# Scaling the delta rule's values on GpSimd instead of VectorE in a two-block fp32 transformer kernel

## The reference, cut to what matters

```python
qkv = jax.nn.silu(causal_short_conv(g_qkv, conv_w))
gq, gk, gv = jnp.split(qkv, [GDN_QK_DIM, 2 * GDN_QK_DIM], axis=-1)
gq = l2_normalize(gq.reshape(B, S, GDN_HEADS, GDN_HEAD_K)) * (GDN_HEAD_K ** -0.5)
gk = l2_normalize(gk.reshape(B, S, GDN_HEADS, GDN_HEAD_K))
beta = jax.nn.sigmoid(g_b.astype(jnp.float32))
...
k_beta = k * beta[..., None]
a_mat = jnp.where(strict, jnp.einsum('bhnid,bhnjd->bhnij', k_beta, k) * decay, 0.0)
lhs = a_mat + jnp.eye(C, dtype=f32)
rhs = jnp.concatenate([v * beta[..., None], k_beta * jnp.exp(g_cum)[..., None]], axis=-1)
sol = lax.linalg.triangular_solve(lhs, rhs, left_side=True, lower=True, unit_diagonal=True)
```

## Time and profile before

| | |
|---|---|
| time, median of 3 runs | 929.16 us (928.70 to 929.86) |
| profiled execution, its own time | 928.95 us |
| its span, first to last instruction | 927.0 us |
| PE busy | 896.3 us (97%) |
| DVE busy | 574.6 us (62%) |
| ACT busy | 511.9 us (55%) |
| POOL busy | 90.7 us (10%) |
| mean granted TensorE clock | 1.000 |

### The profile page before, as it was taken

One profiled execution on the slowest core, in us unless ns is written; L12 is line 12 of the kernel. 1 busy time (PEld: TensorE's weight loads), 2 busy tenths in 40 slices (PEclk: granted clock), 3 DMA queues, 4 the chain that ended last, 5 costly groups with the idle time before them and its releaser, 6 DMA issues. The chain is left out here.

```text
span 927.0 us, 14627 instructions
## 1 busy us (share of the span) xinstructions
PE 896.3 (97%) x5672; PEld 795.1 (86%) x5672; DVE 574.6 (62%) x903; ACT 511.9 (55%) x934; POOL 90.7 (10%) x113
## 2 busy tenths in 40 slices
PE   5999999999999999998999999998999999999998
PEld 5998977888899998887878889977899789998886
DVE  5446556664676664446657988889655676665333
ACT  4465666664665544336468668796255465554331
POOL 1010000000000000001000512240152101000000
PEclk9999999999999999999999999999999999999999
DMA  9756333464455565655454644353340365655552
GB/s 340 250 182 228 95 134 101 148 228 92 147 173 184 183 203 198 203 188 182 136 183 151 196 143 145 104 173 121 88 168 1 110 206 172 184 189 185 182 185 87
DMA packets 110379, 152.22 MB, mean 164 GB/s; under 512 B 6736, under 2 KB 68328, under 8 KB 109928
## 3 DMA queue, kind: packets, MB, share of 16 engines
q1 hardware_dynamic: 110312, 151.31, 50.5%
HBM read 147.99 MB, written 3.30 MB: 163 GB/s over the span
## 5 line engine op out<-in xcount | busy, mean ns | idle before, releaser
L400 DVE TENSOR_TENSOR s_w_lo<-s_w_raw,s_w_hi 128x2048 fp32r<-128x2048 f32 (+1 forms) x198 | 312.4, 1595 | 174.9 <-ACT s_w_hi L394 174.6
L394 ACT ACTIVATE s_w_hi<-s_w_raw 128x2048 fp32r<-128x2048 f32 (+1 forms) x198 | 262.8, 1346 | 152.7 <-PE acc L452 101.9
L462 PE MATMUL acc<-s_h_hi,s_w_hi 128*128 128x256 f32 x800 | 228.0, 285 | 1.9 <-DVE s_h_lo L686 1.9
L464 PE MATMUL acc<-s_h_hi,s_w_lo 128*128 128x256 f32 x800 | 226.3, 283 | 0.0
L463 PE MATMUL acc<-s_h_lo,s_w_hi 128*128 128x256 f32 x800 | 226.3, 283 | 0.0
L462 PEld LDWEIGHTS acc<-s_h_hi,s_w_hi 128*128 128x128 f32 x800 | 153.3, 192 | 2.7 <-DVE s_w_lo L400 1.2
L463 PEld LDWEIGHTS acc<-s_h_lo,s_w_hi 128*128 128x128 f32 x800 | 153.4, 192 | 0.3
L464 PEld LDWEIGHTS acc<-s_h_hi,s_w_lo 128*128 128x128 f32 x800 | 153.3, 192 | 0.0
L452 PE MATMUL acc<-s_w_hi,s_hid_lo 128*128 128x512 f32 x224 | 88.3, 394 | 0.0
L451 PE MATMUL acc<-s_w_lo,s_hid_hi 128*128 128x512 f32 x224 | 87.8, 392 | 0.0
L450 PE MATMUL acc<-s_w_hi,s_hid_hi 128*128 128x512 f32 x224 | 86.9, 388 | 0.0
(11 more groups left out here) (319 smaller groups left out, 1431.0 us busy)
## 6 DMA issues: line engine op xcount, KB each, us to landing
s_w_raw<-in_w_in SPq DMA_DIRECT2D x44, 1024.0 KB, 5.2
s_w_raw<-in_w_ff SPq DMA_DIRECT2D x32, 1024.0 KB, 5.1
s_w_raw<-in_w_mlp_up SPq DMA_DIRECT2D x16, 1024.0 KB, 5.5
s_w_raw<-in_w_mlp_down SPq DMA_DIRECT2D x16, 1024.0 KB, 5.0
s_w_raw<-in_w_out SPq DMA_DIRECT2D x8, 1024.0 KB, 5.3
s_w_raw<-in_w_mk SPq DMA_DIRECT2D x4, 1024.0 KB, 5.1
s_w_raw<-in_w_mv SPq DMA_DIRECT2D x4, 1024.0 KB, 5.0
s_w_raw<-in_w_mq SPq DMA_DIRECT2D x4, 1024.0 KB, 5.0
```

Source lines behind the costliest of these rows:

```text
L394: act.activation(w_hi[u % SPLIT_SLOTS][:, cs], w_raw[u % RAW_SLOTS][:, cs], ACT.Copy).then_inc(w_hi_done, 4 if q is None else 1)
L400: dve.tensor_tensor(w_lo[u % RAW_SLOTS][:, cs], w_raw[u % RAW_SLOTS][:, cs], w_hi[u % SPLIT_SLOTS][:, cs].bitcast(F32), ALU.subtract).then ...
L462: pe.matmul(o, wh[:, cs], hi[:, k, :], start=k == 0, stop=False)
L464: i = pe.matmul(o, wl[:, cs], hi[:, k, :], start=False, stop=k == KC - 1)
```

## The change

The two multiplications of `vb` by beta leave VectorE's stream. GpSimd does them, as the same two 128 x 1024 operations, after `tok_rms_pool(1)` and before `inv_pool`. They report on a semaphore of their own, `vb_done`, and TensorE waits for it before the first matmuls that read `vb`.

```diff
-            else:
-                dve.wait_ge(tok_copied, 12)
-                dve.tensor_tensor(vb[:, n], vb[:, n], per_head(BETA[:, n, :]), ALU.mult).then_inc(tok_done, 1)
+
+        def vb_pool(pool, n):
+            pool.wait_ge(tok_copied, 12)
+            pool.tensor_tensor(vb[:, n], vb[:, n], per_head(BETA[:, n, :]), ALU.mult).then_inc(vb_done, 1)
...
                 if k == 0:
+                    pe.wait_ge(vb_done, NT)
                     pe.wait_ge(u_copied, u_event(0, LEVELS, g))
...
             tok_rms_pool(pool, 1)
+            pool.wait_ge(g2_eg, 2)
+            for n in range(NT):
+                vb_pool(pool, n)
             for n in range(NT):
                 inv_pool(pool, n)
...
             gate_tick(6)
-            for k in range(4, 8):
+            for k in range(4, 6):
                 tok_scale_dve(dve, k)
             kdec_dve(dve)
```

More of the change, by code:

```diff
@@ L365, in build_program @@
         conv_done, conv2_done, tanh_done, qkv_done = [sem(n) for n in ("conv_done", "conv2_done", "tanh_done", "qkv_done")]
-        gate_tanh, tok_mm, tok_copied, tok_sq, tok_ss, tok_rms, tok_done = [sem(n) for n in (
-            "gate_tanh", "tok_mm", "tok_copied", "tok_sq", "tok_ss", "tok_rms", "tok_done")]
+        gate_tanh, tok_mm, tok_copied, tok_sq, tok_ss, tok_rms, tok_done, vb_done = [sem(n) for n in (
+            "gate_tanh", "tok_mm", "tok_copied", "tok_sq", "tok_ss", "tok_rms", "tok_done", "vb_done")]
         back_mm, back_copied, dt_add, dt_done, kdec_done, ap_mm, ap_done = [sem(n) for n in (
```

## The result

The changed kernel takes 931.35 us (median of 19 runs, 930.26 to 933.15) where before takes 929.47 us (19 runs, 927.96 to 931.22): ratio 1.0022, 95% interval 1.0015 to 1.0028, so slower by 0.22%; the two medians differ by 1.88 us. The profiled execution took 931.26 us, its span is 929.4 us.

A forecast was written before the change was run, and what follows sets the result against it. The stage was taken to be bound by VectorE's gapless work up to the masking of A. Removing vb gives -2.27 us, two GpSimd turns +4.68 us: 928.95 + 2.41 = 931.4 us, range for 8 in 10 929.4 to 933.8 us.

The forecast's parts named there:

- vb lay on the path: VectorE ahead of the masking of A: the vb scaling is in the chain of waits, its removal worth -2.27 us.
- GpSimd and VectorE take turns by whole instructions, twice, ahead of the masking: GpSimd's two vb operations each hold up VectorE, at the second kb and the weight split: +4.68 us together.
- A turn costs 2.34 us: VectorE's loss to each GpSimd vb operation: 2.54 us of operation less 0.20 us; allowed range 2.04 to 2.54 us.
- Clock kept: Forecast case: TensorE's clock stays at 2.4 GHz through its 5.39 us idle before the qh transposes; 931.4 us, chance 0.45.
- clock dropped: Rival: after TensorE's 5.39 us idle the qh transposes take 3.65 instead of 2.42 us; 932.3 to 932.8 us, chance 0.26.
- Both ways to the meeting slip alike: TensorE's stream and the chain of DMAs and inversion, meeting at 667.78 us, both slip by 2.41 us.
- The total: Whole kernel: 928.95 us of the profiled execution + 2.41 us of later masking = 931.4 us; slower 0.70.
- Faster: Rival: GpSimd's turns cost VectorE nothing, so the gain is the 2.27 us removed; 926.7 us, chance 0.12.
- no change: Rival: VectorE's operations with a broadcast operand (kb, qh) do not contend, others do; +0.7 us, 929.6 us, chance 0.10.
- Dearer: Rival: GpSimd slower on the broadcast operand, a turn costs 3.1 us; +3.9 us, 932.9 us, chance 0.07.

The follow-up runs named there:

- no_vb: The changed kernel with the scaling of vb left out altogether, TensorE waiting for ScalarE's copies instead: 927.07 us, ratio to before 0.9972.
- dve_late: The kernel before, with the two vb operations still on VectorE but behind the masking of A and the second weight split after it: 927.58 us, ratio 0.9969.
- pool_late: The changed kernel, with GpSimd also waiting for a_done 4, so its two vb operations start only after the masking of A: 927.27 us, ratio to before 0.9970.
- pool_write: The changed kernel with GpSimd's two multiplications replaced by memsets of vb, which write SBUF and read nothing: 927.47 us, ratio to before 0.9975.
- pool_plain: The changed kernel with GpSimd multiplying vb by a plain 128x1024 operand (the residual x) in place of spread beta: 932.21 us, ratio to before 1.0028.
- pe_fill: The changed kernel with 32 extra identity transposes where TensorE waits for the masking: 931.34 us, ratio to before 1.0020; repeated, 930.62 us, 1.0013.
- split_late: Against dve_late, the weight split between kdec and the masking (gate_tick(7)) moved directly behind the masking: 924.47 us, ratio to before 0.9950.
- vb_last: As split_late, but the vb pair stands still later on VectorE, behind the second masking: 925.59 us, ratio to before 0.9960.
- after_again: The changed kernel itself, timed and profiled once more: 931.90 us, ratio to before 1.0024.

## Why the prediction was right, step by step

- **vb lay on the path.** Right. Without it, or with it anywhere behind the masking, the kernel is 2.1 to 2.9 us faster (no_vb, dve_late, pool_late), where 2.27 us were forecast for the removal; between the marks it is 2.35 to 2.63 us.
- **GpSimd and VectorE take turns by whole instructions, twice, ahead of the masking.** Right, and at the places forecast: the second kb and the split each wait for one GpSimd operation. That VectorE has two SBUF inputs is not enough; GpSimd has to read as well (pool_write). The Trainium skill, SBUF — State Buffer, section Who interferes with whom, says the same, that a GpSimd instruction which only writes does not contend, and the trace agrees: kb kept 2.35 us. That VectorE's second input is needed too is argued from the rows, since all its operations that were stopped have one; no run took it away.
- **A turn costs 2.34 us.** This is the term that was mis-sized: it costs 1.70 us, under the 2.04 to 2.54 us that I had allowed it. I had taken 2.54 us for the operation from masks and additions whose second operand has a value of its own in each of 128 or more columns; with one beta for 128 columns GpSimd needs 1.91 us. With a full operand a turn costs 2.25 and 2.18 us (pool_plain). The difference of turn and operation, 0.20 us, was right (1.91 - 1.70 = 0.21). So the sum should have been 3.40 - 2.27 = +1.13 us in place of +2.41 us, and the masking came 1.13 us late.
- **Clock kept, 0.45, against clock dropped, 0.26.** The less likely of the two happened, and already with a wait of 4.12 us, not the 5.39 us that I had given it. The transposes take 3.65 us, exactly the number from the earlier trace rows, in the first profile, and 3.15 us in the second. The mean granted clock was 0.994 to 0.998 in each of the 19 runs. The Trainium skill, TensorE: Matmul & The Clock Gate, section What's actually happening, has the rule that activity releases the throttle; here the trace agrees: 32 transposes put into the wait kept the clock at 1.00.
- **Both ways to the meeting slip alike.** Not so once the clock falls: the masking and the DMAs slip by 1.13 us, TensorE by 3.11 us up to the second set of A's products (line 1683 at 656.26 us, 652.79 us before, less 0.36 us of a later first mark): 1.14 us by the later start of the qh transposes, the other 1.97 us by the slower transposes and gate matmuls. 1.73 us of this reach the second mark. The 0.34 us of idle at the meeting were not all the slack that TensorE had; a second idle of before, 0.41 us at 683.67 us, is gone after the change as well, and what took up the rest was not traced.
- **The total.** 931.4 us was forecast and 931.35 us measured, but out of errors that nearly cancel. The turns were put 1.28 us too high. The clock stood at nothing in this case and cost 0 to 1.3 us. And the sum started from one profiled execution at 928.95 us, where the median of 19 is 929.47 us. The change itself was forecast at +2.41 us and is +1.88 us between the medians, of which 1.13 us are the later masking; that the other 0.75 us are the clock's fits pe_fill but is not measured by itself. The sign was earned by the turns, the last digit was luck.
- **The rivals.** Faster (GpSimd's turns for nothing) and no change (operands spread over columns don't contend) are refuted by kb's 4.06 us: kb itself has such an operand. Dearer had the wrong sign: with the spread operand GpSimd took 1.91 us, with the full one about 2.4 us. Clock is the rival that came true in part: it was to be added to turns of 2.34 us and came with turns of 1.70 us.

## What to carry to other kernels

Work moved from VectorE to GpSimd need not be off VectorE's path: while GpSimd reads SBUF, VectorE's operations with two SBUF inputs wait for it. Here 2.27 us went away and 3.40 us of turns came back. Ask first what in the stage has to be early, and move work behind it on the same engine: the pair put behind the masking on VectorE gained 2.1 us, and with the weight split put there as well it was 4.5 us between the marks (4.6 us by the ratio of split_late, 3.7 us by that of vb_last). A wait of TensorE that grows by one microsecond can cost more than that microsecond, since the clock may be at half when it starts again or fall just after it has.

## What the runs showed of the hardware that was not expected

- A GpSimd multiplication of 128 x 1024 float32 works 1.91 us when its second operand is one value per 128 columns, and about 2.4 us when it is a full tile; the masks of the earlier trace rows come to 2.48 ns for a column, these to 1.87 and about 2.4 ns.
- A GpSimd memset of 128 x 1024 (0.92 us each) passes beside a two-input VectorE operation without any cost to VectorE (kb 2.35 us). What it takes by itself no run shows.
- TensorE's clock was at 1.00 through a wait of 2.98 us in the profiled execution of before. It fell before the end of waits of 4.12 (the changed kernel), 4.11 and 5.15 us, and with TensorE already at work again behind waits of 4.12 (after_again) and 3.55 us; the 16 transposes took 3.65, 3.64, 3.49, 3.15 and 2.88 us against 2.42 us.
- A mean clock of 0.998 does not name its place. In the profiled executions of dve_late and pool_write it comes from the stretch from 80 to 100 us (0.91), and the stage has 1.00. Of the 31 timed executions of before beside the first four kernels, 27 have a mean of 0.998 or less, of the 12 of dve_late 6 and of the 7 of pool_late none. So the wait of 2.98 us may cost before some clock in executions that were not profiled; no trace shows it.
